# One score product for two key groups of a running sequence, in a one-core decoder step

## The chip, the cores and the metric

The kernel runs on one core of a Trainium2 chip. The metric is the device time of one execution in microseconds (us). TensorE (PE) multiplies, VectorE (DVE) and ScalarE (ACT) work on tiles, GpSimd (POOL) issues the gathers from memory, and SyncE (SP) issues the plain transfers.

## The reference

The reference is one step of a decoder layer: projections, a linear attention, a differential softmax attention, an output projection and a mixture of experts, for a new prompt of 1,024 tokens and for 8 running sequences with 4 new tokens each. The change touches one part of it, the attention of the running sequences over their 8,192 past tokens, whose keys and values lie in pages:

```python
k_past = cache_k[page_table, :, l].reshape(DB, past, DIFF_HEADS, 2 * DIFF_DQK)
v_past = cache_v[page_table, :, l].reshape(DB, past, DIFF_HEADS, DIFF_DV)
...
s = jnp.concatenate([diff_scores(q, k_past), diff_scores(q, k_new)], axis=-1)
...
p = jax.nn.softmax(jnp.where(mask, s, -jnp.inf), axis=-1)
return p[:, :, 0] - lam * p[:, :, 1]
```

Everything is in 32-bit floats. The keys and values of the past are 8 x 8,192 x 512 numbers each, 134 MB each.

## The kernel before, in words

The function `mixers` holds the attention of the running sequences, the linear attention and the attention of the prompt. They run side by side on the same engines, in an order that a list of slots sets.

A running sequence ("sample" b, 0 to 7) has 16 groups of keys and 16 of values. A group is 512 tokens: 128 partitions x 2,048 numbers, 1 MB. Each group takes one slot of the list `slots`. For samples 1 to 7 the list is K0 K1 K2 K3 V0 K4 V1 K5 K6 V2 K7 V3 K8 V4 K9 K10 V5 K11 V6 K12 K13 V7 K14 V8 K15, then V9 to V15, where K are the sample's keys and V the values of the sample before. For sample 0 there are the 16 keys and six empty slots; after sample 7's round its own values come last.

The groups live in a ring of seven places in SBUF (`RING = 7`); load number n, in the order of the slots, goes to place n mod 7. POOL issues the loads in that order at L790, one gather of 1 MB each, and before load n it waits until the group of load n - 7 has been used up. So a place that is given back late holds up all the loads behind it on POOL.

A key group passes DVE first: `turn_keys` (L1330) turns it in place, in 32x32 blocks. Then `scores` on PE (L810) multiplies it: 4 blocks of 32 numbers by 4 heads, 16 products of 128 columns, each with 32 stationary columns that fill one strip of the array and one strip of 32 PSUM partitions. (The trace records each of these 32-bit products twice, as two passes, so 32 records for a group.) Four groups fill the PSUM bank `SC`, and ACT copies it to `d_s` (`keep_scores`, L1101). After the 16th group come the maximum, the exponentials and the turning of the scores (`turn`), which PE writes to the same bank. A value group is multiplied by `values` (L846) in 16 products.

Each engine walks the slots. In step n DVE turns the key group of slot n, and PE does the product of the group of slot n - 1 and then the pieces that the linear attention (`linear`) and the prompt's attention (`attention`) have in that step. PE works through its list strictly in order, so a wait in `scores` holds up all of these.

`s_kt` counts turned key groups, `s_sc` key groups whose products are done, `s_pv` the same for values, `s_cp` the copies of the bank and `s_tk` the turned pieces of scores that ACT has taken away.

Of the kernel before, what the change touches and what calls it, by code (L numbers as in the profile page):

```python
# [15 lines left out]
P = 128  # L16
# [7 lines left out]
HEADS, DK, DV, RANK = 4, 64, 128, 16  # L24
# [7 lines left out]
GROUP = 4  # L32
GROUPS = PAGES // GROUP
# [107 lines left out]
def const(k, name, rows=P):  # L141
    a, n = CONST_AT[name]
    return k.ident[0:rows, 0:n] if name == "ident" else k.consts[0:rows, a - P:a - P + n]
# [439 lines left out]
def mixers(nc, k, io):  # L583
# [10 lines left out]
    RING, GAP = 7, 6  # L594
    BLOCKS = 2 * DK // 32
# [5 lines left out]
    SC, OUT = 0, 1  # L601
    TURN, LIN_OUT = (5, 6), 7
    ATT_T, ATT_O = 6, 7
    KEYS, VALUES = "keys", "values"
# [14 lines left out]
    at = {what: n for n, what in enumerate(slots) if what}  # L619
    loads = [what for what in slots if what]  # L620
    load_no = {what: n for n, what in enumerate(loads)}
# [3 lines left out]
    start, total = [], 0  # L625
# [11 lines left out]
    with ExitStack() as ctx:  # L637
        def sb(name, shape, dt=F32):
            return ctx.enter_context(nc.sbuf_tensor(name, shape, dt))

        sem = k.sem
        ring = sb("d_ring", [P, RING, GROUP * W])
# [3 lines left out]
        qb = sb("d_qb", [P, 2, BLOCKS, HEADS, 32])  # L646
# [20 lines left out]
        def carve(a, *shape):  # L667
# [30 lines left out]
        s_kt, s_sc, s_cp, s_nm, s_exp, s_t, s_tk, s_pv = (sem("d_kt_"), sem("d_sc"), sem("d_cp"), sem("d_nm_"), sem("d_exp"),  # L698
                                                          sem("d_t_"), sem("d_tk"), sem("d_pv"))
# [18 lines left out]
        def arrived(eng, what):  # L718
            n = load_no[what]
            eng.wait_ge(s_load[n % RING], 16 * (n // RING + 1))  # L720

        def in_ring(what):
            return ring[:, load_no[what] % RING]
# [10 lines left out]
        with nc.Block() as block:  # L734
# [45 lines left out]
            @block.gpsimd  # L780
            def _(pool):
                pool.wait_ge(s_rows, 1)
                for n, (kind, b, x) in enumerate(loads):
                    if loads[n] == (VALUES, 0, 0):
                        pool.wait_ge(s_rows, 2)
                    if n >= RING:
                        was, b0, x0 = loads[n - RING]
                        pool.wait_ge(s_sc if was == KEYS else s_pv, b0 * GROUPS + x0 + 1)
                    index = rows[:, 0 if kind == KEYS else 1, b, x:x + 1].bitcast(U32)
                    pool.indirect_dma_start(out=ring[:, n % RING], out_offset=None, in_=caches[kind],  # L790
                                            in_offset=bass.IndirectOffsetOnAxis(ap=index, axis=0)).then_inc(s_load[n % RING], 16)

            @block.tensor
            def _(pe):
                ident = const(k, "ident")

                def scores(b, x):
                    n = b * GROUPS + x
                    pe.wait_ge(s_kt, n + 1)
                    pe.wait_ge(s_qb, b + 1)  # L800
                    if x % 4 == 0:
                        if n:
                            pe.wait_ge(s_cp, n // 4)
                        if x == 0 and b:
                            pe.wait_ge(s_tk, b * PIECES)
                    part = slice(P * (x % 4), P * (x % 4) + P)
                    keys = in_ring((KEYS, b, x)).rearrange("p (r h i j) -> p r h i j", r=GROUP, h=HEADS, i=BLOCKS)
                    for i in range(BLOCKS):
                        for h in range(HEADS):
                            mm = pe.matmul(k.ps[32 * h:32 * h + 32, SC, part], qb[:, b % 2, i, h, :], keys[:, :, h, i, :],  # L810
                                           start=i == 0, stop=i == BLOCKS - 1)
                    mm.then_inc(s_sc, 1)

                def turn(b, x):
                    n = b * PIECES + x
                    pe.wait_ge(s_exp, n + 1)
                    if n:
                        pe.wait_ge(s_tk, n)
                    if x == 0:
                        mm = pe.transpose(k.ps[0:NS, SC, 0:P], s_new[:, b, :], ident)  # L820
                    else:
                        for r in range(GROUP):
                            a = 512 * (x - 1) + r * P
                            mm = pe.transpose(k.ps[:, SC, r * P:(r + 1) * P], s[:, a:a + P], ident)
                    mm.then_inc(s_t, 1)

                def open_sums(b):
                    pe.wait_ge(s_exp, (b + 1) * PIECES)
                    pe.wait_ge(s_tk, b * PIECES + 1)
                    if b:  # L830
                        pe.wait_ge(s_ok, b)
                    pe.matmul(k.ps[:, OUT, 0:DV + PIECES], alike[:], sz[:, b % 2, :], start=True, stop=False, skip_group_check=True)
                    for h in range(HEADS):
                        pe.matmul(k.ps[32 * h:32 * h + 8, OUT, 0:DV], pTn[:, 32 * h:32 * h + 8], k.new_v[:, h * DV:(h + 1) * DV],
                                  start=False, stop=False, skip_group_check=True)

                def values(b, x):
                    if x == 0:
                        open_sums(b)
                    pe.wait_ge(s_tk, b * PIECES + x // 4 + 2)  # L840
                    arrived(pe, (VALUES, b, x))
                    v = in_ring((VALUES, b, x)).rearrange("p (r n) -> p r n", r=GROUP)
                    a = x % 4
                    for r in range(GROUP):
                        for h in range(HEADS):
                            mm = pe.matmul(k.ps[32 * h:32 * h + 8, OUT, 0:DV],  # L846
                                           pT[:, (b * SUPERS + x // 4) % KEPT_P, r, 32 * h + 8 * a:32 * h + 8 * a + 8],
                                           v[:, r, h * DV:(h + 1) * DV], start=False, stop=x == GROUPS - 1 and r == GROUP - 1,
                                           skip_group_check=True)
                    mm.then_inc(s_pv, 1)  # L850

                def running(n):
                    for b in range(SAMPLES):
                        if n - at[KEYS, b, GROUPS - 1] in (4, 5, 6):
                            turn(b, 2 * (n - at[KEYS, b, GROUPS - 1] - 4))
                    if n and slots[n - 1]:
                        kind, b, x = slots[n - 1]
                        scores(b, x) if kind == KEYS else values(b, x)
                    for b in range(SAMPLES):
                        if n - at[KEYS, b, GROUPS - 1] in (4, 5):  # L860
                            turn(b, 2 * (n - at[KEYS, b, GROUPS - 1] - 4) + 1)
# [211 lines left out]
                for i in range(BLOCKS):  # L1073
                    part = slice(32 * i, 32 * i + 32)
                    mm = pe.matmul(k.ps[:, 2 + i, 0:P], spread[part], k.qTs[part].rearrange("p h t -> p (h t)"), start=True, stop=True)
                mm.then_inc(s_qp, 1)
                pe.wait_ge(s_qd, 1)
                for b in range(SAMPLES):
                    for h in range(HEADS):
                        mm = pe.matmul(k.ps[32 * h:32 * h + 32, OUT, b * NS:(b + 1) * NS], q_pad[:, b, h, :], k.kTs[:, h, :],  # L1080
                                       start=True, stop=True)
# [11 lines left out]
            def _(act):  # L1093
                def keep_scores(b, x):
                    n = b * SUPERS + x
                    act.wait_ge(s_sc, 4 * (n + 1))
                    if n == 0:
                        act.wait_ge(s_nq, 1)
                    if x == 0 and b:
                        act.wait_ge(s_t, b * PIECES)  # L1100
                    act.copy(s[:, 512 * x:512 * (x + 1)].rearrange("p (r t j) -> p t r j", r=GROUP, t=4),  # L1101
                             k.ps[:, SC, :].rearrange("p (t r j) -> p t r j", t=4, r=GROUP)).then_inc(s_cp, 1)
# [164 lines left out]
            def _(dve):  # L1267
# [27 lines left out]

                def queries(b):
                    if b >= 2:
                        dve.wait_ge(s_sc, (b - 1) * GROUPS)
                    mine = const(k, "mine").rearrange("p (i x) -> p i x", i=BLOCKS)
                    for i in range(BLOCKS):  # L1300
                        q = spread_q[:, i].rearrange("p (h n) -> p h n", h=HEADS)[:, :, STEPS * b:STEPS * (b + 1)]
                        ins = dve.tensor_tensor(qb[:, b % 2, i].rearrange("p h (x t) -> p h x t", t=STEPS),
                                                q.unsqueeze(2).to_broadcast([P, HEADS, 8, STEPS]),
                                                mine[:, i].unsqueeze(1).unsqueeze(3).to_broadcast([P, HEADS, 8, STEPS]), ALU.mult)
                    ins.then_inc(s_qb, 1)
# [1130 lines left out]
```

## Time and profile before

| what | value |
|---|---|
| median of 3 runs | 1993.85 us (1989.64 to 1997.44) |
| the profiled execution, its own time | 1993.27 us |
| its span, first to last instruction | 1991.4 us |
| PE busy | 1675.7 us (84%) |
| DVE busy | 1267.2 us (64%) |
| ACT busy | 831.9 us (42%) |
| POOL busy | 401.4 us (20%) |
| read from and written to HBM | 531.41 MB and 43.81 MB |
| key products on PE, L810 | 163.4 us busy, first at 376.7 us, last at 1039.5 us |
| value products on PE, L846 | 146.4 us busy, first at 468.0 us, last at 1092.7 us |
| turning of keys on DVE, L1330 | 292.2 us busy |

Busy times are those in which at least one instruction of the group ran. An engine's busy share over the whole span is a mean over stages with different limits: the ring's loads run from 363.8 to 1076.3 us, and only what the profile shows there bears on the change. The DMA share that the views give is the mean busy share of the 16 DMA engines.

### The profile page before, as it was taken

The page shows a single profiled execution, that of the slowest core. Times are in us where ns is not written, and L with a number is a line of the kernel's source. Part 1 is how long each engine was busy: PE and PEld are TensorE (multiplying, and loading weights), DVE is VectorE, ACT ScalarE, POOL GpSimd, SP SyncE. Part 2 cuts the span into 40 slices and gives each one's busy share as a digit, 9 for nine tenths or more (in the row PEclk, how much of TensorE's full clock was granted, in tenths as well). Part 3 has the DMA queues.
Part 4 walks back from the last instruction along what each step waited for, and adds up shares of the span by engine and source line. Part 5 has one row for each costly group of instructions (what it writes and reads, how often), then busy time and mean ns, then how long its engine had stood idle before and what let it go on. Part 6 is the DMA issues. An engine that isn't in the chain of part 4 may idle for free. (4 is left out here: it accounts for less than half of the span.)

```text
span 1991.4 us, 37111 instructions
## 1 busy us (share of the span) xinstructions
PE 1675.7 (84%) x14983; PEld 1280.3 (64%) x14983; DVE 1267.2 (64%) x1685; ACT 831.9 (42%) x1415; POOL 401.4 (20%) x362
## 2 busy tenths in 40 slices
PE   6999999478888888877777699708999999999990
PEld 4677777356777756555555255406888888888870
DVE  4321441578687588678782233347898889888954
ACT  4322222012322143343332322116778778777850
POOL 0000000212333243333332000031221222022103
PEclk9999999668999798798989799758999999999995
DMA  6062121887999899999998541008999999999957
GB/s 203 11 249 89 43 77 45 294 298 284 376 366 417 311 417 417 388 414 407 417 406 363 171 190 64 22 19 334 392 401 407 404 403 403 406 403 405 402 203 272
DMA packets 105169, 577.14 MB, mean 290 GB/s; under 512 B 14913, under 2 KB 20417, under 8 KB 52049
## 3 DMA queue, kind: packets, MB, share of 16 engines
q0 software_dynamic: 46512, 302.28, 37.9%
q1 hardware_dynamic: 58528, 272.98, 35.3%
q8 instruction: 101, 1.65, 0.3%
q14 instruction: 28, 0.22, 0.0%
HBM read 531.41 MB, written 43.81 MB: 289 GB/s over the span
## 5 line engine op out<-in xcount | busy, mean ns | idle before, releaser
L2020 DVE TENSOR_TENSOR e_l<-first_w,e_h 128x1024 fp32r<-128x1024 f32 x256 | 294.6, 1222 | 10.0 <-ACT e_h L2017 9.6
L1330 DVE STREAM_TRANSPOSE d_ring<-d_ring 128x2048 f32<-128x2048 f32 x128 | 292.2, 2298 | 11.8 <-DMA d_ring<-in_cache_k,d_rows 11.1
L2017 ACT CAST e_h<-first_w 128x1024 fp32r<-128x1024 f32 x256 | 250.3, 1048 | 83.8 <-POOLq L2089 42.8
L810 PE MATMUL ps<-d_ring,d_qb 128*32 128x128 f32 x4096 | 163.4, 311 | 103.8 <-DVE d_ring L1330 103.6
L790 POOL DMA_INDIRECT d_ring<-in_cache_k,d_rows x128 | 122.9, 960 | 533.2 <-DVE d_rows L1283 265.0
L810 PEld LDWEIGHTS ps<-d_ring,d_qb 128*32 128x32 f32 x4096 | 124.0, 124 | 136.8 <-DVE d_ring L1330 113.0
L1979 PE MATMUL ps<-e_h,e_xh 128*128 128x512 f32 x512 | 206.7, 404 | 3.5 <-DVE e_xl L2029 3.5
L1981 PE MATMUL ps<-e_h,e_xl 128*128 128x512 f32 x512 | 203.7, 398 | 0.0
L1980 PE MATMUL ps<-e_l,e_xh 128*128 128x512 f32 x512 | 203.6, 398 | 0.0
L321 PE MATMUL ps<-wh,xh 128*128 128x512 f32 (+1 forms) x432 | 173.7, 402 | 0.0
L322 PE MATMUL ps<-wl,xh 128*128 128x512 f32 (+1 forms) x432 | 171.1, 396 | 0.0
L323 PE MATMUL ps<-wh,xl 128*128 128x512 f32 (+1 forms) x432 | 171.1, 396 | 0.0
L2097 POOL COPY e_row<-order 128x1 uint32 x32 | 85.2, 2662 | 420.1 <-PE ps L1987 414.1
L790 POOL DMA_INDIRECT d_ring<-in_cache_v,d_rows x128 | 121.9, 952 | 200.4 <-PE ps L846 105.2
L2026 DVE TENSOR_TENSOR e_l<-first_w,e_h 128x1024 fp32r<-128x1024 f32 x128 | 148.3, 1222 | 8.1 <-ACT e_h L2023 8.1
L846 PE MATMUL ps<-d_ring,d_pT 128*8 128x128 f32 x4096 | 146.4, 289 | 7.4 <-DMA d_ring<-in_cache_v,d_rows 7.2
L1651 PE MATMUL ps<-m_wout,m_catT 128*128 128x512 f32 (+1 forms) x288 | 130.3, 612 | 1.7 <-ACT m_catT L1698 1.4
L846 PEld LDWEIGHTS ps<-d_ring,d_pT 128*8 128x8 f32 x4096 | 107.5, 94 | 32.9 <-issue 23.6
L2023 ACT CAST e_h<-first_w 128x1024 fp32r<-128x1024 f32 x128 | 124.9, 1059 | 0.0
L1979 PEld LDWEIGHTS ps<-e_h,e_xh 128*128 128x128 f32 x512 | 97.5, 190 | 26.1 <-DVE e_xl L2029 3.2
L1981 PEld LDWEIGHTS ps<-e_h,e_xl 128*128 128x128 f32 x512 | 97.0, 189 | 23.5
L1980 PEld LDWEIGHTS ps<-e_l,e_xh 128*128 128x128 f32 x512 | 97.2, 190 | 22.0
(314 smaller groups left out, 2698.3 us busy)
## 6 DMA issues: line engine op xcount, KB each, us to landing
first_w<-in_w_down SPq DMA_DIRECT2D x32, 2048.0 KB, 9.0
first_w<-in_w_up SPq DMA_DIRECT2D x62, 1024.0 KB, 8.1
first_w<-in_w_gate SPq DMA_DIRECT2D x62, 1024.0 KB, 10.9
ys_d<-e_y SPq DMA_DIRECT2D x32, 512.0 KB, 10.0
cat<-in_w_in SPq DMA_DIRECT2D x6, 2048.0 KB, 9.6
ys_d<-cat POOLq DMA_DIRECT2D x1, 8192.0 KB, 33.5
kT<-in_x_prompt SPq DMA_DIRECT2D x8, 512.0 KB, 6.8
m_wout<-in_w_out SPq DMA_DIRECT2D x2, 2048.0 KB, 10.0
```

What stands on the lines that cost most here:

```text
L321: pe.matmul(out, xh[:, kk, cols_], w_high[:, kk, :], start=first, stop=False)
L322: pe.matmul(out, xh[:, kk, cols_], w_low[:, kk, :], start=False, stop=False)
L323: return pe.matmul(out, xl[:, kk, cols_], w_high[:, kk, :], start=False, stop=last)
L790: pool.indirect_dma_start(out=ring[:, n % RING], out_offset=None, in_=caches[kind], in_offset=bass.IndirectOffsetOnAxis(ap=index, axis=0)) ...
L810: mm = pe.matmul(k.ps[32 * h:32 * h + 32, SC, part], qb[:, b % 2, i, h, :], keys[:, :, h, i, :], start=i == 0, stop=i == BLOCKS - 1)
L846: mm = pe.matmul(k.ps[32 * h:32 * h + 8, OUT, 0:DV], pT[:, (b * SUPERS + x // 4) % KEPT_P, r, 32 * h + 8 * a:32 * h + 8 * a + 8], v[:, r, ...
L1330: dve.transpose(in_ring((KEYS, b, g)), in_ring((KEYS, b, g))).then_inc(s_kt, 1)
L1979: pe.matmul(out, high, w_high, start=first, stop=False)
L1980: pe.matmul(out, high, w_low, start=False, stop=False)
L1981: return pe.matmul(out, low, w_high, start=False, stop=last)
L2017: return act.copy(h13[:, :, kk, :], w13[:, :, kk, :])
L2020: return dve.tensor_tensor(l13[:, :, kk, :], w13[:, :, kk, :], h13[:, :, kk, :].bitcast(F32), ALU.subtract)
```

## The change

PE no longer multiplies each key group in the step after its own slot. It does nothing for an even group (K0, K2, ...) and multiplies it together with the odd one behind it. Where the ring place of the even group has the lower number, one product takes both groups as its moving operand, 256 columns with the distance of the places as a stride. Where the ring has wrapped between the two, each group has its own product of 128 columns, one after the other. With the list of slots above, the places are in order in 50 of the 64 pairs. `s_sc` rises once for a pair, and the waits on it (POOL's for a free place, ACT's for the bank, DVE's for the queries' buffer) are halved to match. The number of slots, the loads and their order, the ring, and the work of DVE and ACT stay.

```diff
                     if n >= RING:
                         was, b0, x0 = loads[n - RING]
-                        pool.wait_ge(s_sc if was == KEYS else s_pv, b0 * GROUPS + x0 + 1)
+                        if was == KEYS:
+                            pool.wait_ge(s_sc, (b0 * GROUPS + x0) // 2 + 1)
+                        else:
+                            pool.wait_ge(s_pv, b0 * GROUPS + x0 + 1)
...
-                    if x % 4 == 0:
-                        if n:
+                    if x % 4 == 1:
+                        if x > 1 or b:
                             pe.wait_ge(s_cp, n // 4)
-                        if x == 0 and b:
+                        if x == 1 and b:
                             pe.wait_ge(s_tk, b * PIECES)
-                    part = slice(P * (x % 4), P * (x % 4) + P)
-                    keys = in_ring((KEYS, b, x)).rearrange("p (r h i j) -> p r h i j", r=GROUP, h=HEADS, i=BLOCKS)
-                    for i in range(BLOCKS):
-                        for h in range(HEADS):
-                            mm = pe.matmul(k.ps[32 * h:32 * h + 32, SC, part], qb[:, b % 2, i, h, :], keys[:, :, h, i, :],
-                                           start=i == 0, stop=i == BLOCKS - 1)
+                    places = [load_no[KEYS, b, g] % RING for g in (x - 1, x)]
+                    first = P * ((x - 1) % 4)
+                    if places[0] < places[1]:
+                        products = [(ring[:, places[0]:places[1] + 1:places[1] - places[0]], slice(first, first + 2 * P))]
+                    else:
+                        products = [(ring[:, at:at + 1], slice(first + P * y, first + P * y + P)) for y, at in enumerate(places)]
+                    for two, part in products:
+                        keys = two.rearrange("p y (r h i j) -> p y r h i j", r=GROUP, h=HEADS, i=BLOCKS)
+                        for i in range(BLOCKS):
+                            for h in range(HEADS):
+                                mm = pe.matmul(k.ps[32 * h:32 * h + 32, SC, part], qb[:, b % 2, i, h, :], keys[:, :, :, h, i, :],
+                                               start=i == 0, stop=i == BLOCKS - 1)
                     mm.then_inc(s_sc, 1)
...
-                        scores(b, x) if kind == KEYS else values(b, x)
+                        if kind == VALUES:
+                            values(b, x)
+                        elif x % 2:
+                            scores(b, x)
...
-                    act.wait_ge(s_sc, 4 * (n + 1))
+                    act.wait_ge(s_sc, 2 * (n + 1))
...
-                        dve.wait_ge(s_sc, (b - 1) * GROUPS)
+                        dve.wait_ge(s_sc, (b - 1) * GROUPS // 2)
```

How this moves PE's list is seen at two places. The first is in the round of sample 4, from V0 to V2. L810 is the product of a key group, L846 that of a value group, and L1025, L1039 and L1055 are pieces of the prompt's attention. In the kernel before, PE's list reads:

```order
1661 L846 MATMUL ps<-d_ring,d_pT 8x128 x16
1662 L810 MATMUL ps<-d_ring,d_qb 32x128 x16
1663 L846 MATMUL ps<-d_ring,d_pT 8x128 x16
1664 L1025 MATMUL ps<-kT,qT 128x512 x4
1665 L810 MATMUL ps<-d_ring,d_qb 32x128 x16
1666 L1039 MATMUL ps<-ident,z 16x128
1667 L1039 MATMUL ps<-ident,z 128x128
1668 L810 MATMUL ps<-d_ring,d_qb 32x128 x16
1669 L1055 MATMUL ps<-meta_dv,a_turned 128x128
1670 L1055 MATMUL ps<-x_scratch,a_turned 128x128
1671 L846 MATMUL ps<-d_ring,d_pT 8x128 x16
1672 L810 MATMUL ps<-d_ring,d_qb 32x128 x16
```

In the changed kernel the same stretch of PE's list reads as follows; its lines are 9 to 12 higher (L819 is the key product, L855 the value product, L1037, L1051 and L1067 the prompt's pieces).

```order
1636 L855 MATMUL ps<-d_ring,d_pT 8x128 x32
1637 L1037 MATMUL ps<-kT,qT 128x512 x4
1638 L819 MATMUL ps<-d_ring,d_qb 32x128 x32
1639 L1051 MATMUL ps<-ident,z 16x128
1640 L1051 MATMUL ps<-ident,z 128x128
1641 L1067 MATMUL ps<-meta_dv,a_turned 128x128
1642 L1067 MATMUL ps<-x_scratch,a_turned 128x128
1643 L855 MATMUL ps<-d_ring,d_pT 8x128 x16
1644 L819 MATMUL ps<-d_ring,d_qb 32x256 x16
```

K4 (row 1662 before) now stands behind V1 and behind the prompt's piece, beside K5; this pair has wrapped in the ring and keeps 128 columns. K6 (row 1668 before) stands behind V2, in one product of 256 columns with K7.

The second place is in the round of sample 3, around a long piece of the prompt's attention on PE (L1012 before, L1024 after: 64 products against the meta tokens' keys). Before, PE's list reads:

```order
1586 L846 MATMUL ps<-d_ring,d_pT 8x128 x16
1587 L810 MATMUL ps<-d_ring,d_qb 32x128 x16
1588 L1012 MATMUL ps<-meta_kT,qT 128x16 x64
1589 L810 MATMUL ps<-d_ring,d_qb 32x128 x16
1590 L846 MATMUL ps<-d_ring,d_pT 8x128 x16
1591 L1025 MATMUL ps<-kT,qT 128x512 x4
1592 L810 MATMUL ps<-d_ring,d_qb 32x128 x16
1593 L846 MATMUL ps<-d_ring,d_pT 8x128 x16
```

and after:

```order
1569 L855 MATMUL ps<-d_ring,d_pT 8x128 x16
1570 L819 MATMUL ps<-d_ring,d_qb 32x256 x16
1571 L1024 MATMUL ps<-meta_kT,qT 128x16 x64
1572 L855 MATMUL ps<-d_ring,d_pT 8x128 x16
1573 L1037 MATMUL ps<-kT,qT 128x512 x4
1574 L819 MATMUL ps<-d_ring,d_qb 32x256 x16
1575 L855 MATMUL ps<-d_ring,d_pT 8x128 x32
```

K6 (row 1589 before), which was the first product behind the long piece, now stands behind V2 and the next piece of the prompt's attention.

## Rows read from the trace of the kernel before

**Rows 1.** The page: the span, and the DMA share in 40 slices (tenths).

```profile
span 1991.4 us, 37111 instructions
...
DMA  6062121887999899999998541008999999999957
```

**Rows 2.** Busy times by stretch: PE, PEld, DVE, ACT, POOL; granted clock, DMA share, GB/s.

```profile
440.00:460.00 20.00, 12.12 (x113) 9.27 (x112) 11.80 (x20) 10.42 (x25) 1.50 (x2) 0.64 0.22 84
...
460.00:700.00 240.00, 209.48 (x3599) 174.75 (x3597) 175.54 (x211) 58.39 (x136) 81.51 (x85) 0.93 0.93 369
700.00:1090.00 390.00, 308.63 (x5720) 225.69 (x5723) 279.14 (x441) 138.41 (x445) 140.66 (x149) 0.90 1.00 409
```

**Rows 3.** Waits, 460 to 1090 us: total us, times, longest.

```profile
POOL d_ring L790 <- PE ps L810: 243.0, 98, 22.1
POOL d_ring L790 <- PE ps L846: 153.3, 98, 7.0
...
PE ps L810 <- DVE d_ring L1330: 80.6, 49, 4.3
...
DVE d_ring L1330 <- DMA d_ring<-in_cache_k,d_rows: 7.9, 7, 2.0
...
PE ps L846 <- DMA d_ring<-in_cache_v,d_rows: 6.6, 5, 1.9
```

**Rows 4.** Groups by line, 460 to 1090 us: busy, mean ns, idle before.

```profile
L810 PE MATMUL ps<-d_ring,d_qb 128*32 128x128 f32 x3552 | 135.7, 301 | 80.8 <-DVE d_ring L1330 80.6
L790 POOL DMA_INDIRECT d_ring<-in_cache_v,d_rows x126 | 120.0, 953 | 190.7 <-PE ps L846 105.2 <-PE ps L810 78.8 <-issue 6.7
...
L790 POOL DMA_INDIRECT d_ring<-in_cache_k,d_rows x107 | 102.7, 960 | 220.6 <-PE ps L810 164.1 <-PE ps L846 48.1 <-issue 8.4
```

**Rows 5.** The ring's loads, line L790, whole trace: issue to landing.

```profile
DMA to landing us min/median/max: 5.7/9.9/19.9
```

**Rows 6.** Timeline of PE in sample 4's round: start, duration, instructions [idle before].

```profile
740.50 1.06 PE L810 MATMUL ps<-d_ring,d_qb 128*32 128x128 f32 x32
741.38 1.06 PE L846 MATMUL ps<-d_ring,d_pT 128*8 128x128 f32 x32
...
744.28 1.08 PE L810 MATMUL ps<-d_ring,d_qb 128*32 128x128 f32 x32
...
746.80 1.08 PE L810 MATMUL ps<-d_ring,d_qb 128*32 128x128 f32 x32 [1.13 <-DVE d_ring L1330]
...
748.65 1.06 PE L846 MATMUL ps<-d_ring,d_pT 128*8 128x128 f32 x32
...
752.43 1.93 PE L810 MATMUL ps<-d_ring,d_qb 128*32 128x128 f32 x32 [2.72 <-DVE d_ring L1330]
...
764.86 1.95 PE L810 MATMUL ps<-d_ring,d_qb 128*32 128x128 f32 x64
```

**Rows 7.** Timeline of POOL in the same stretch.

```profile
742.23 0.94 POOL L790 DMA_INDIRECT d_ring<-in_cache_k,d_rows  x1 [0.30 <-issue]
743.48 0.94 POOL L790 DMA_INDIRECT d_ring<-in_cache_v,d_rows  x1 [0.30 <-issue]
745.66 0.94 POOL L790 DMA_INDIRECT d_ring<-in_cache_k,d_rows  x1 [1.25 <-PE ps L810]
748.19 0.94 POOL L790 DMA_INDIRECT d_ring<-in_cache_k,d_rows  x1 [1.59 <-PE ps L810]
750.01 0.94 POOL L790 DMA_INDIRECT d_ring<-in_cache_v,d_rows  x1 [0.89 <-PE ps L846]
754.67 0.94 POOL L790 DMA_INDIRECT d_ring<-in_cache_k,d_rows  x1 [3.72 <-PE ps L810]
```

**Rows 8.** Timeline of PE: products of 256 columns, then of 128.

```profile
643.00 0.60 PE L922 MATMUL ps<-x_scratch 128*128 128x256 f32 x2
643.43 1.50 PE L927 MATMUL ps<-cat,x_scratch 128*128 128x128 f32 x12
644.86 1.06 PE L846 MATMUL ps<-d_ring,d_pT 128*8 128x128 f32 x32
```

## The prediction

> **What bounds the kernel now.** I began with the page. Its DMA digits [rows 1] fall in the middle third of the span, where the ring's loads run, almost all at 8 and 9: there memory traffic, and not PE, looks like the limit. The busy times by stretch [rows 2] say how far. From 700 to 1090 us the 16 DMA engines are at a share of 1.00 and move 409 GB/s; from 460 to 700 us they are at 0.93, so 0.07 x 240 = 17 us of DMA time are lost there. PE is busy 309 of 390 us in the second stretch and DVE 279: both have room. Only short pieces fall out of this, such as 440 to 460 us with a DMA share of 0.22, behind the first sample's maximum.
>
> The waits [rows 3] show how the engines hang together. POOL waits 243 us for a key product and 153 us for a value product: it always has the next load ready and wants a ring place. So the number of loads under way is set by how fast places come back. A load takes 9.9 us from issue to landing at the median and 5.7 us at least [rows 5]; 126 + 107 = 233 loads are issued in 630 us [rows 4], one in 2.70 us, which is the pitch of the stage. Hence 9.9 / 2.7 = 3.7 of the seven places are in flight and the rest hold landed groups. The load that took 5.7 us shows that a good part of 9.9 us is queueing: 9.9 - 5.7 = 4.2 us is the **cover**, by which an issue may come later before the DMA engines run dry.
>
> **The change part by part.**
>
> *Products.* A key group takes 1.08 us at the full clock and 1.93 us at the half [rows 6]. Two groups back to back take 1.95 us in 64 records, so the second one adds 0.87 us. A product of 256 columns on 32 stationary columns is not in the trace. The nearest rows have 128 stationary columns [rows 8]: two records of 256 columns go from 643.00 to 643.43 us, 0.215 us each, and twelve of 128 from 643.43 to 644.86, 0.119 us each. One of 256 for two of 128 thus saves 0.238 - 0.215 = 0.023 us, a tenth, and by it a pair takes 1.93 us instead of 2 x 1.08 = 2.16 us apart: 0.23 us saved, 0.85 us behind the time that the odd group alone would end. In 50 ordered pairs that is 50 x 0.2 = 10 us of PE time; the 14 wrapped pairs only move together. I put this at nothing: PE idles 81 us before key products for want of a turned group [rows 3, 4], and the DMA engines are full. Were PE on the path, the 10 us would come off. So the ends are -10 and 0, and I take 0.
>
> *Copies and softmax.* ACT's copy of the bank, the maximum and the exponentials hang on the same odd groups as before, 0.85 us later. At the borders of samples 1 to 7 the values V9 to V15 lie beside that chain and hide it. At sample 0 nothing does (440 to 460 us, [rows 2]): +1 us, once.
>
> *The hold.* This is the main term. An even key's place now stays taken until the pair is done, and POOL, strictly in order, stays behind it with loads whose places are already free. The stretch in rows 6 and 7 shows it. K4 ends at 741.56, V1 at 742.44 and K5 at 745.36 us [rows 6]; POOL refills their places at 742.23, 743.48 and 745.66 us [rows 7], 0.30 us behind a product, or 1.25 us behind its own last issue. After the change K4 and K5 both end at 745.36 + 0.85 = 746.21, so the three issues come at 746.5, 747.8 and 749.0: 4.3, 4.3 and 3.3 us later. K6, V2 and K7 end at 747.88, 749.71 and 754.36; their refills, at 748.19, 750.01 and 754.67, move to 755.5, 756.8 and 758.0: 7.3, 6.8 and 3.3 us later, and up to a microsecond more where the clock is at its half level, as for this K7.
>
> In pitches: an even key with a value between it and its partner is late by 2 x 2.70 + 0.85 = 6.25 us; the value by 2.70 + 0.85 + 1.25 = 4.8; the odd key by 0.85 + 2 x 1.25 = 3.35; an even key right beside its partner by 2.70 + 0.85 = 3.55, and that partner by 2.1. The round of a sample has five pairs of the first kind and three of the second. Over its 32 loads the mean delay is (5 x 6.25 + 5 x 4.8 + 5 x 3.35 + 3 x 3.55 + 3 x 2.1) / 32 = 2.8 us, within the cover of 4.2 us. Only the even keys of the first kind exceed it clearly, by 6.25 - 4.2 = 2.05 us; the value's 0.6 us of excess falls into the same gap, since the transfers queue. In 7 samples that is 35 x 2.05 = 72 us of possible gaps in the DMA traffic.
>
> Not all of it reaches the end, because landed groups lie in the ring as a second cover. DVE sat idle for a landing in 7 key groups and PE in 5 values [rows 3]: 12 of 233 loads, 5%, and 5% of 72 is 4 us. PE waited for a turned group 49 times in 3552 / 32 = 111 groups [rows 3, 4]: 44%, and 44% of 72 is 32 us. These are the ends. The trace does not settle the share between them. The turning on DVE is the first to feel a late landing, and it rarely waited, so I take a value nearer to the low end, 11 us (the geometric mean of 4 and 32).
>
> By the Trainium skill (DMA: Bandwidth & Descriptors, "Anatomy of one DMA — SWDGE (gpsimd) path") a GpSimd transfer costs about 2.0 us plus its bytes at 436 GB/s. For 1 MB that is 4.4 us, an estimate from that page; the cover would be 5.5 us, the excess 0.75 us, the gaps 26 us and the term 4 us instead of 11, for 1998 us in all. No load here landed in under 5.7 us [rows 5], so I keep the trace's figure.
>
> **Sum.** 1993.27 us (the profiled execution, 0.6 us below the median of the runs) + 0 + 1 + 11 = **2005 us**.
>
> **The rivals.**
>
> *The ring absorbs it.* The mean delay of 2.8 us is within the cover, and DVE waits for landings only 8 us in all [rows 3]. With the low end the sum is 1993.27 + 1 + 4 = 1998 us, and with PE's 10 us on the path 1988. Against it: with the DMA share at 1.00 [rows 2], whatever gap opens between 700 and 1090 us cannot be made up.
>
> *Faster.* PE no longer stops at even keys, where half of its 81 us of waiting would lie if it is spread evenly, and what stands behind these products in its list (attention, the values) starts sooner. The ring gains if the time from landing to product falls by more than the 2.8 us by which refills come late; that is the point from which it decides. What can be won is the 17 us that the DMA engines lose between 460 and 700 us: 1976 us with all of it, 1985 with half. For it speaks PE's strict order; against it, that POOL's order returns the value's place no earlier than the even key's, and that PE's waits come back at the odd key.
> The Trainium skill (TensorEngine Tiling (Array Packing), "Instruction Overhead") gives each matmul about 60 cycles of overhead, 25 ns at 2.4 GHz. With 32 records fewer in 50 pairs that is an estimate of 40 us of PE work, and 1953 us if PE set the pace. Rows 8 agree with such a saving per product (23 ns), but four strips work side by side, and rows 2 show the DMA engines as the bound; I give this reading 0.02 of the rival's 0.14.
>
> *All of the gaps count.* If the ring holds too little landed work behind each gap, between 32 and 72 us are lost: 2026 to 2066 us. For it: seven places, of which a waiting pair with a value holds three. Against it: the two covers above.
>
> *The change does little of what it says.* 14 of 64 pairs fall back to two products, and the saving per column is a tenth. This is already in the first term and changes no sum.
>
> **How the numbers follow.** Forecast (part of the gaps count, 2002 to 2026): 0.42. Absorbed (1988 to 2002): 0.30. Faster: 0.14. All gaps: 0.14. Half a per cent, 10 us, is about what a measurement of this kernel can tell from no change: above 2003.8 lie three quarters of the forecast's case and all of the heaviest, 0.47; below 1983.9 nearly all of the faster case, 0.13; between them 0.40. For 8 in 10 the range cuts the outer part of the faster case and the outer part of the heaviest: 1985 to 2032. The forecast's own range is 2002 to 2026.
>
> **What would show it.** The DMA share from 700 us to the end of the ring's loads should fall from 1.00 to about 0.97, the median from issue to landing from 9.9 to about 7 us, and the last value product should end about 12 us later than now; all stages behind it should take as long as before. POOL's issues should come in bursts of three, 1.25 us apart, and its waits for value products should shrink in favour of key products. A pair's product of 32 records should take about 1.93 us. The prediction is wrong if the landing time falls and the DMA share stays (the covers suffice), if the landing-to-product time shrinks by more than 3 us (faster), or if a pair takes much longer than 1.93 us.

## The result, and the profile after

The changed kernel takes 2052.48 us in the median of 4 runs (2047.81 to 2068.98), against 1994.76 us before: 1.0307 times as long, with a 95% interval of 1.0243 to 1.0372. The profiled execution took 2056.62 us. The prediction was 2005 us with a range of 1985 to 2032; the rival "all of the gaps count", 2026 to 2066 us, is where it came out.

First the page of the changed kernel: the span, and the group of the key products (busy us, mean ns | idle before).

```profile
span 2054.7 us, 33847 instructions
...
L819 PE MATMUL ps<-d_ring,d_qb 128*32 128x256 f32 (+1 forms) x2496 | 164.0, 423 | 102.7 <-DVE d_ring L1342 102.5
```

The records of key products fell from 4096 to 2496, the time in which they run did not (163.4 us before).

Where the 63 us of span lie is seen by cutting at the last value product, at 1092.8 us before and 1152.7 us after. Busy times by stretch of the kernel before (PE, PEld, DVE, ACT, POOL; clock, DMA share, GB/s):

```profile
460.00:1092.80 632.80, 520.31 (x9357) 401.84 (x9359) 454.68 (x651) 196.80 (x580) 222.17 (x233) 0.91 0.97 392
...
1092.80:1991.40 898.60, 758.60 (x3283) 572.58 (x3275) 625.78 (x691) 515.30 (x603) 154.01 (x100) 0.91 0.74 294
```

and of the changed kernel:

```profile
460.00:700.00 240.00, 199.06 (x2751) 152.93 (x2754) 165.72 (x194) 54.32 (x121) 73.80 (x76) 0.89 0.87 340
700.00:1090.00 390.00, 287.77 (x4338) 191.88 (x4334) 276.13 (x417) 125.07 (x403) 130.18 (x138) 0.86 0.92 365
...
460.00:1152.70 692.70, 537.69 (x8014) 381.15 (x8013) 457.98 (x652) 196.76 (x580) 221.78 (x233) 0.87 0.90 358
...
1152.70:2054.70 902.00, 759.27 (x3279) 572.72 (x3271) 625.57 (x691) 514.85 (x603) 155.74 (x100) 0.91 0.74 293
```

The stages behind the ring take 902.0 us instead of 898.6. Of the 63 us, 60 thus lie between 460 us and the last value product, which is the ring's stage. From 460 us on it moves the same data, 632.8 x 392 = 692.7 x 358 = 248 thousand us x GB/s, or 248 MB, at a lower rate. From 700 to 1090 us, where the DMA share was 1.00 [rows 2], it is 0.92. By the rates, an estimate from these rows, (369 - 340) x 240 = 7 MB or 17 us at 409 GB/s are lost from 460 to 700 us, and (409 - 365) x 390 = 17 MB or 42 us from 700 to 1090 us.

The waits of the changed kernel, 460 to 1150 us (total us, times, longest), answer to [rows 3]:

```profile
POOL d_ring L793 <- PE ps L819: 346.5, 55, 25.0
...
PE ps L819 <- DVE d_ring L1342: 85.0, 31, 5.8
POOL d_ring L793 <- PE ps L855: 76.4, 50, 5.8
...
DVE d_ring L1342 <- DMA d_ring<-in_cache_k,d_rows: 35.6, 29, 3.5
```

POOL's waits have moved to the key products, and there are fewer and longer ones: 346.5 / 55 = 6.3 us each instead of 243 / 98 = 2.5. DVE now waits for a landing 29 times and not 7.

One such wait close by. POOL, from 722 to 737 us:

```profile
722.47 0.94 POOL L793 DMA_INDIRECT d_ring<-in_cache_v,d_rows  x1 [0.30 <-issue]
734.67 0.93 POOL L793 DMA_INDIRECT d_ring<-in_cache_v,d_rows  x1 [11.26 <-PE ps L819]
735.91 0.94 POOL L793 DMA_INDIRECT d_ring<-in_cache_v,d_rows  x1 [0.30 <-issue]
737.15 0.94 POOL L793 DMA_INDIRECT d_ring<-in_cache_v,d_rows  x1 [0.30 <-issue]
```

PE at the same time:

```profile
725.22 1.02 PE L1051 MATMUL ps<-ident,z 128*16 128x128 f32 x4 [3.71 <-DVE z L1539]
726.17 1.90 PE L855 MATMUL ps<-d_ring,d_pT 128*8 128x128 f32 x32
...
731.15 3.21 PE L819 MATMUL ps<-d_ring,d_qb 128*32 128x256 f32 x32
```

And the stretch in steps of 3 us (clock, DMA share, GB/s are the last three columns):

```profile
724.00:727.00 3.00, 1.78 (x22) 1.23 (x26) 3.00 (x2) 0.62 (x2) 0.00 (x0) 0.50 1.00 421
727.00:730.00 3.00, 3.00 (x29) 2.24 (x21) 0.38 (x1) 0.00 (x0) 0.00 (x0) 0.50 1.03 429
730.00:733.00 3.00, 3.00 (x26) 1.75 (x29) 0.00 (x0) 0.58 (x1) 0.00 (x0) 0.50 0.73 295
733.00:736.00 3.00, 3.00 (x49) 1.96 (x45) 0.87 (x3) 0.85 (x2) 1.02 (x2) 0.87 0.02 8
```

POOL stands 11.26 us before the place of an even key. A value product ends at 726.17 + 1.90 = 728.07 us, 6.6 us before POOL issues anything, but in POOL's order its place comes behind that of the even key. The pair ends at 731.15 + 3.21 = 734.36 us, mostly at the half clock, and three loads follow 1.25 us apart. In the meantime the DMA engines have run dry: share 0.02 from 733 to 736 us. The hold is not alone here: PE stood 3.71 us before a piece of the prompt's attention (L1051), and only behind it come the value and the pair. In the kernel before, this pair's even key, K14 of sample 3, was multiplied ahead of that piece (L1039 there), and the piece did not wait:

```profile
703.95 1.93 PE L810 MATMUL ps<-d_ring,d_qb 128*32 128x128 f32 x32 [2.73 <-DVE d_ring L1330]
705.81 1.02 PE L1039 MATMUL ps<-ident,z 128*16 128x128 f32 x4
```

### The profile page after: what moved, and what is told of

Read it like the earlier page. It is cut to its first block and busy times, and to the rows that moved or that the text cites. A ratio compares the mean times of both kernels' runs of the same rounds, so it can differ in the third digit from the quotient of the medians.

```text
span 2054.7 us, 33847 instructions
## 1 busy us (share of the span) xinstructions
PE 1691.5 (82%) x13383; PEld 1250.3 (61%) x13383; DVE 1269.4 (62%) x1685; ACT 831.0 (40%) x1415; POOL 401.7 (20%) x362
## 5 line engine op out<-in xcount | busy, mean ns | idle before, releaser
L819 PE MATMUL ps<-d_ring,d_qb 128*32 128x256 f32 (+1 forms) x2496 | 164.0, 423 | 102.7 <-DVE d_ring L1342 102.5
L819 PEld LDWEIGHTS ps<-d_ring,d_qb 128*32 128x32 f32 x2496 | 86.9, 133 | 160.7 <-DVE d_ring L1342 115.4
L855 PE MATMUL ps<-d_ring,d_pT 128*8 128x128 f32 x4096 | 144.9, 288 | 9.9 <-DMA d_ring<-in_cache_v,d_rows 9.7
L855 PEld LDWEIGHTS ps<-d_ring,d_pT 128*8 128x8 f32 x4096 | 105.9, 94 | 38.5 <-issue 28.6
```

What stands on the lines that cost most here:

```text
L855: mm = pe.matmul(k.ps[32 * h:32 * h + 8, OUT, 0:DV], pT[:, (b * SUPERS + x // 4) % KEPT_P, r, 32 * h + 8 * a:32 * h + 8 * a + 8], v[:, r, ...
```

## The experiments

All ratios are to the kernel before, timed on the same chip, with 95% intervals. They are not the quotients of the medians, from which they differ by up to 0.2%. Losses in us below are those of the ratios, at 1994 us, unless medians are named.

| run | median us | ratio | interval |
|---|---|---|---|
| changed kernel | 2052.48 | 1.0307 | 1.0243 to 1.0372 |
| hold alone | 2025.99 | 1.0166 | 1.0139 to 1.0192 |
| pairs of two 128-column products | 2055.28 | 1.0298 | 1.0267 to 1.0329 |
| all pairs adjacent | 2045.59 | 1.0241 | 1.0204 to 1.0279 |
| kernel before with those slots | 2023.31 | 1.0158 | 1.0124 to 1.0192 |
| even product ahead of the wait | 2037.11 | 1.0220 | 1.0179 to 1.0261 |
| hold alone, odd products twice | 2049.54 | 1.0267 | 1.0221 to 1.0313 |
| hold alone, places in order of return | 2008.11 | 1.0064 | 1.0046 to 1.0083 |
| six places | 2007.49 | 1.0061 | 1.0040 to 1.0082 |
| five places | 2045.10 | 1.0254 | 1.0223 to 1.0285 |
| changed kernel, places in order of return | 2036.63 | 1.0199 | 1.0158 to 1.0240 |
| the same, even product ahead of the wait | 2022.50 | 1.0122 | 1.0092 to 1.0152 |
| close pairs alone | 2005.05 | 1.0064 | 1.0038 to 1.0089 |

**The hold alone.**

```diff
-pool.wait_ge(s_sc if was == KEYS else s_pv, b0 * GROUPS + x0 + 1)
+pool.wait_ge(s_sc if was == KEYS else s_pv, b0 * GROUPS + (x0 | 1 if was == KEYS else x0) + 1)
```

> The kernel before with one edit: POOL waits, for the place of an even key group, until the products of the odd group behind it are done. The products stay single, of 128 columns, each in its own step. Theory H (the ring places that come back late are the cost): most of the changed kernel's loss of 58 us, 2035 to 2060 us, a DMA share of 0.88 to 0.94 from 700 to 1090 us. Rival O (PE's new order is the cost: even products moved behind other work, waits at odd keys that hold up the prompt's pieces): within 10 us of the kernel before, 1985 to 2005. Rival P (products of 256 columns from two places are slow): the same, 1985 to 2005.

It cost 1.66%, 33 us: less than theory H expected, far more than O or P allowed. Theory H also missed the DMA share from 700 us: 0.98 (the row stands below) and not 0.88 to 0.94. A little over half of the loss, by the central values (1.66 of 3.07%), thus comes from ring places that POOL must wait for, with PE's work and order as before.

**Two 128-column products for every pair.**

```diff
-                    if places[0] < places[1]:
+                    if False:
```

> The changed kernel with two products of 128 columns for every pair, one after the other in the odd group's step; order, places and waits as in the changed kernel. H: as slow as the changed kernel, 2042 to 2062. O: the same. P: the loss goes, 1990 to 2010.

At 1.0298 it cannot be told from the changed kernel. The width of the products is not the cost, and theory P falls. It is worth little the other way as well. In this run's profile key products ran for 170.0 us, against 164.0 us in the changed kernel's:

```profile
L819 PE MATMUL ps<-d_ring,d_qb 128*32 128x128 f32 x4096 | 170.0, 335 | 105.4 <-DVE d_ring L1342 105.4
```

Even these 6 us need not be the width, for the granted clock from 700 to 1090 us was 0.82 here and 0.86 there. The trace of the changed kernel has both widths at both clock levels, x32 with 256 columns and x64 with 128:

```profile
782.90 3.64 PE L819 MATMUL ps<-d_ring,d_qb 128*32 128x256 f32 x32 [3.61 <-DVE d_ring L1342]
794.35 1.95 PE L819 MATMUL ps<-d_ring,d_qb 128*32 128x128 f32 x64
892.05 3.64 PE L819 MATMUL ps<-d_ring,d_qb 128*32 128x128 f32 x64 [3.51 <-DVE d_ring L1342]
```

At the full clock 256 columns take 1.93 us (the row is in the part on the prediction) and two products of 128 take 1.95 us; at the half both take 3.64 us. The difference between this run and the one before it, 1.32%, is what the hold does not explain.

**All pairs adjacent, and its control.**

```diff
-            slots += early[max(0, (x - 2) * len(early) // 14):max(0, (x - 1) * len(early) // 14)]
+            slots += early[max(0, (x - 3) * len(early) // 14):max(0, (x - 1) * len(early) // 14)] if x % 2 else []
```

> The changed kernel with another list of slots: the values that lay between the two groups of a pair now follow the pair, so each even place is held for one pitch of 2.7 us and not two. H as the prediction had it (only holds beyond the cover of 4.2 us cost): 1994 to 2004. H where the cover is not there and the loss goes with the mean delay of the refills (1.4 us instead of 2.8): half the loss, 2018 to 2030. O: nearly the whole loss stays, over 2035.

> The kernel before with the list of slots of the run on adjacent pairs, as its control. All theories: within 10 us of the kernel before, 1985 to 2005; the difference of the two runs is then the cost of pairing adjacent groups.

The control itself is 1.58% slower, against every expectation, so the first run's time says little by itself. Against its control it costs 0.8%, 17 us in 64 pairs (22 us by the medians). Pairing adjacent groups is not free. This run does not tell how much of that is the hold of one pitch, and how much the pair's later end or the even product's place in PE's list.

**The even product ahead of the wait for the odd group.**

```diff
-                    pe.wait_ge(s_kt, n + 1)
+                    pe.wait_ge(s_kt, n)
...
-                    if places[0] < places[1]:
+                    if False:
...
-                    for two, part in products:
+                    for y, (two, part) in enumerate(products):
+                        if y:
+                            pe.wait_ge(s_kt, n + 1)
```

> The run with pairs of two 128-column products, but in the odd group's step PE does the even group's product before it waits for the turning of the odd group, so that behind this wait only one product is left. Places come back as late as in the run with the hold alone (2026 us), and the even product stands as late in PE's list as in the run with two 128-column products (2055 us). Theory E (the 29 us between those two runs come from the pair's end, which lies a product behind an odd group's own end): 2018 to 2035. Theory O (they come from PE's order, the even product behind a value and pieces of the prompt): 2045 to 2060.

2037 us lies between what the two theories expected. Of the 1.32% it takes back 0.78%, about 16 us (its interval lies below that of the run with two products): this is the part of the pair's late end. About 11 us (0.54%) stay; here the intervals of this run and of the hold alone overlap.

The traces show what the edit does to a pair's end. From the end of an odd group's turning to the end of its product (means over the 56 odd groups from 460 to 1150 us, worked out from the records of one trace each) it took 2.1 us in the kernel before, 2.3 us with the hold alone, 3.6 us with two products behind the wait, and 2.5 us here. In the changed kernel it took 3.5 us.

**The hold alone, with every odd group's product done twice.**

```diff
-                    for i in range(BLOCKS):
+                    for again in range(1 + x % 2):
+                        for i in range(BLOCKS):
...
```

> The run with the hold alone, and PE does every odd group's product twice, the second time over the first with the same result. An odd group then ends as late behind its wait as a pair does, but the even product stays in its own step. E: 2045 to 2062. O: 2020 to 2035.

2050 us, as theory E expected: with the even product in its old place in PE's list, a product more between the odd group's turning and the return of the places costs 1.0%, 20 us or so. The time from turning to end, as above, was 3.2 us. This run also adds work to PE, so it prices the late end only roughly. It answers a rival too, that the change costs time because the granted clock falls (from 0.90 to 0.86, 700 to 1090 us). Here the clock rose to 0.93, and the loss is 53 us all the same:

```profile
700.00:1090.00 390.00, 307.86 (x6342) 236.22 (x6342) 285.82 (x426) 126.27 (x411) 131.80 (x141) 0.93 0.95 376
```

**The hold alone, with places taken in the order in which they come back.**

```diff
+    given_back = []
+    for kind, b, x in loads:
+        if kind == VALUES:
+            given_back.append((kind, b, x))
+        elif x % 2:
+            given_back += [(kind, b, x - 1), (kind, b, x)]
...
+        place[what] = n if n < RING else place[given_back[n - RING]]
...
-                        was, b0, x0 = loads[n - RING]
+                        was, b0, x0 = given_back[n - RING]
```

> The run with the hold alone, but a load takes the ring place that comes back next, and not the place of the load seven earlier: a value between two held keys gives its place to the next load at once. The number of places and the hold are the same. By pitches the mean delay of a refill falls from 2.2 to 1.4 us. If POOL's strict queue behind a held place carries its share: 2008 to 2020. If only the held places count: 2020 to 2030 as in the run with the hold alone.

With the same hold the loss falls from 33 to 13 us. So 20 of the 33 us come from POOL standing before a held place while a value's place is free. The other 13 us are lost although, by the pitches, no refill in this run is late by more than 2.7 us. Busy times by stretch of this run:

```profile
460.00:700.00 240.00, 210.50 (x3553) 176.28 (x3543) 172.82 (x206) 58.42 (x135) 78.22 (x83) 0.91 0.90 358
700.00:1090.00 390.00, 304.63 (x5648) 220.30 (x5644) 284.10 (x447) 138.66 (x447) 142.04 (x151) 0.92 1.00 406
```

and of the run with the hold alone:

```profile
460.00:700.00 240.00, 208.75 (x3446) 175.09 (x3445) 166.07 (x199) 55.68 (x123) 75.88 (x79) 0.89 0.88 348
700.00:1090.00 390.00, 302.22 (x5389) 219.19 (x5392) 284.31 (x443) 136.08 (x441) 136.55 (x145) 0.89 0.98 393
```

From 700 us on the DMA share is 1.00 in the first and 0.98 in the second; from 460 to 700 us it is 0.90 and 0.88, where it was 0.93 [rows 2].

**Six and five places.**

```diff
-    RING, GAP = 7, 6
+    RING, GAP = 6, 6
```

For five places the first number is 5.

> The kernel before with six ring places and not seven. It prices a place: the hold alone delays refills by 2.2 us in the mean, 0.8 of a pitch of 2.70 us, which is 0.8 of a place in seven. If landing time above the least one (9.9 against 5.7 us, 1.6 pitches) is a cover that costs nothing to use, as the prediction had it: 1990 to 2005. If there is no such cover and a place is worth what the hold cost: 2025 to 2045.

> The kernel before with five ring places. A refill then comes two pitches earlier in the ring's turn than with seven: 5.4 us less time for every load, evenly, about twice the mean delay of the changed kernel (2.8 us). If the loss follows the mean time taken from the loads: well over the changed kernel's 58 us, 2070 to 2120. If it follows the unevenness (a few refills late by 6 us and more and POOL's queue behind them, while six places cost only 12 us): below it, 2020 to 2050.

A place less costs 12 us, two cost 50 us. The run with six places lies between its two expectations, near the first: the time taken from the loads was not quite free. One place is 2.7 us less for every load, evenly, and cost 12 us; the hold alone is 2.2 us in the mean, unevenly, and cost 33 us, with intervals apart. Two places are 5.4 us, evenly, and did not cost more than the changed kernel's 2.8 us in the mean, unevenly (50 against 61 us, intervals overlapping). The loss does not follow the mean delay. The landing times, of the run with six places, of that with five and of the changed kernel:

```profile
DMA to landing us min/median/max: 5.9/9.5/19.9
```

```profile
DMA to landing us min/median/max: 5.5/8.9/14.1
```

```profile
DMA to landing us min/median/max: 5.2/9.6/20.9
```

With six places the ring goes round in 6 x 2.70 = 16.2 us and not in 18.9, at the same 233 loads issued from 460 to 1090 us. The median landing time fell by only 0.4 us; by this estimate the other 2.3 us came from the time that landed groups lie in the ring (18.9 - 9.9 = 9.0 us before, 16.2 - 9.5 = 6.7 here).

**The changed kernel with places in order of return, and that with the even product ahead of the wait.** These put the two edits above on the changed kernel.

> The changed kernel, but a load takes the ring place that comes back next and not that of the load seven earlier; the products of 256 columns go where the two places are in order. The same edit took 18 us off the run with the hold alone. If the blocked queue is a part of the changed kernel's loss of its own: 2030 to 2042. If the later end of the pairs (two products behind the wait) also eats this gain: 2042 to 2055. Theory that holds alone count: as the changed kernel, over 2050.

> The changed kernel with two products of 128 columns for a pair, the even one ahead of the wait for the odd group's turning, and with loads that take the ring place that comes back next. Only the hold of the even place and PE's new order are left of the change. If the later end of a pair and the blocked queue are the two large parts of the loss: 2005 to 2022. If PE's new order is a large part of its own: 2025 to 2040.

From 1.0307 the first edit leads to 1.0199 and both to 1.0122. Each takes off what it took off alone (1.1% and 0.8%, against 1.0% and 0.8%). The rest, 0.58% above the hold with places in order of return, with intervals apart (1.0092 to 1.0152 against 1.0046 to 1.0083), is what the even product's later place in PE's list costs. The last run came out half a microsecond above the range for two large parts, and below that for a large part of PE's order. Why the later place costs this is settled only in part. The traces show that pairs still end later: from the odd group's turning to its product's end it took 2.7 us in the last run, against 2.0 us in the hold with places in order of return. The runs do not tell how much of the cost this is and how much is work held up behind the two products.

**Close pairs alone.**

```diff
...
+                    pair = at[KEYS, b, x | 1] == at[KEYS, b, x & ~1] + 1
...
-                    mm.then_inc(s_sc, 1)
+                    mm.then_inc(s_sc, 2 if pair else 1)
```

> The change only where the two groups of a pair follow each other in the list of slots: 29 of the 64 pairs, 25 of them with products of 256 columns; the other keys as in the kernel before. The even place is held for one pitch and a product, 3.55 us, within the 4.2 us that a landing has above the least one. As the prediction had it, that costs nothing and the 0.2 us per pair saved on TensorE is worth nothing: 1988 to 2002. If close pairs cost what they cost in the run with all pairs adjacent (22 us in 64 pairs): 2002 to 2010.

1.0064: about 13 us for 29 pairs, 0.4 us a pair (0.3 to 0.6 by the interval), near the 17 / 64 = 0.3 us of the adjacent pairs. Even the pairs that the prediction held to be free lose, and the saving on PE does not show. No version of the change beat the kernel before.

## Why the prediction was wrong, point by point

**What bounds the kernel** held. The DMA engines are the limit of the stage, the stages behind it kept their time to 3 us, and the loss is a lower transfer rate.

**Products** held: nothing gained, nothing lost by the width; the timeline of the changed kernel has a pair of 256 columns at 1.93 us at the full clock, as estimated:

```profile
717.76 1.93 PE L819 MATMUL ps<-d_ring,d_qb 128*32 128x256 f32 x32 [1.11 <-DVE d_ring L1342]
```

The 0.2 us a pair that this saves against two products apart come from standing back to back and not from the width, for two products of 128 columns back to back take 1.95 us. The second half of a pair was undersized, though. Over all pairs key products take 164.0 / 64 = 2.56 us, against 163.4 / 128 = 1.28 us for a group before, so a pair ends 1.28 us and not 0.85 us behind an odd group. Many run at the lower clock level, as the 3.64 us above: the mean granted clock from 700 to 1090 us is 0.86, and was 0.90.

**The hold** was the right mechanism with the wrong size: 11 us were predicted, and the whole loss is about 60. By steps, as ratios to the kernel before: the held places themselves 0.64%, POOL's queue behind them 1.02%, the even product's later place 0.54%, the pair's late end 0.78%, the width 0.09%, which is not told from nothing: together 3.07%. The first, second and fourth, 49 us, are the effects that the prediction's 72 us of gaps was made of; the third, 11 us, it did not have.

The step that failed is what the two covers were to save, the second above all: "5% of 72 is 4 us", "44% of 72 is 32 us", and a value near the low end. Those shares were the waits of the kernel before, in which refills came one by one. They did not hold for the changed kernel: DVE's waits for landings went from 7 to 29. Nor is their number a measure of the loss: the changed kernel with places in order of return has 11 of them and loses 40 us. From 700 us on the stage was at a DMA share of 1.00, so a gap could not be made up behind it; the prediction said this itself, against its first rival, and did not apply it to its own sum. In place of a sixth of the gap time, 11 of 72 us, the runs put these effects at 49 us. For the hold alone it is 33 us, where the gaps by the same pitches are 35 x (5.40 - 4.2) = 42 us.

The first cover failed too, for delays within it were counted as free. In the hold with places in order of return no refill is later than 2.7 us by the pitches, so the prediction's way of counting finds no gap there; it lost 13 us. Six places, 2.7 us for every load, lost 12 us, and close pairs alone, at 3.55 us, 13 us, though these have the pairs' later products in them too. So of the 33 us of the hold alone about 20 stand for its 42 us of gaps, a half, and the rest is time that the first cover was to hide.

The median from issue to landing was to fall to about 7 us as the first cover was used up; it stayed at 9.6 us while the DMA share fell to 0.92. The trace of the changed kernel shows why. It tells the landing of 134 of the 233 loads issued from 460 to 1150 us. The 23 of these that were issued more than 5.4 us behind the load before them landed in 6.3 us at the median; the 72 issued at most 1.4 us behind it took 10.2 us (in the kernel before there are 5 and 18 such loads). Refills that come in bursts thus queue behind one another and keep the median long, although the engines have run dry before them. And an even delay hardly comes out of the landing time: 0.4 of 2.7 us with six places, 1.0 of 5.4 us with five.

**Copies and softmax** was not tried by itself. Its 1 us stands at sample 0, where ACT's last copy of the bank starts 0.8 us later than before, close to the 0.85 us of the prediction:

```profile
442.03 0.59 ACT L1101 COPY d_s<-ps 128x512 f32<-128x512 f32 x1 [14.16 <-PE ps L810]
```

```profile
442.80 0.58 ACT L1113 COPY d_s<-ps 128x512 f32<-128x512 f32 x1 [17.97 <-PE ps L819]
```

**The rivals.** Absorbed and faster are refuted; PE's waits at key products did not shrink (80.6 us in 49 before, 85.0 us in 31 after), they gathered at the odd keys. The reading of 40 us less PE work for 1600 records fewer did not show either: at equal clock the width changes a pair by 0.02 us at most. All gaps was right in time, though 11 us of the loss come from the even product's later place, which it does not hold. Its reason, little landed work behind each gap, fits the rise of DVE's waits but is not shown by it. Open stays why the list of slots of the adjacent pairs costs 1.58% without any pairing; its trace has only 2 waits of DVE for landings, and a DMA share of 0.97 from 700 us.

**How the numbers follow** has a slip that changes nothing: three quarters of 0.42 and all of 0.14 make 0.455, not 0.47.

## What to carry to other kernels

Where a stage runs at a DMA share near 1.00, a buffer that comes back late costs transfer time that is not made up. Here about half or more of the time beyond the spare landing time came out, and delays within that time were not free. The share of waits in the trace before was no measure of it. Look at the spacing of these returns and not only at their mean: a ring that is filled strictly in order stops at the one place that is late, and a place less for every load (12 us) cost less here than a smaller mean delay in a few late places (33 us). Giving the next load the place that is free next took about 20 us off here without any more memory.

## What the runs showed of the hardware that was not expected

A long median from issue to landing is no proof of full DMA engines: 9.9 us at a share of 1.00 and 9.6 us at 0.92. And products twice as wide on 32 stationary columns saved next to nothing: 1.93 us for 32 records of 256 columns against 1.95 us for 64 of 128 at the full clock, and 3.64 us for either at the half.
